# Sampled stage of a hybrid decoder step: the second state's decay and update moved ahead of the first state's product

## Time and profile before

| | us |
|---|---|
| median of 3 runs (lowest, highest) | 1473.77 (1472.54, 1475.15) |
| the profiled execution, its own time | 1470.45 |
| its span, first to last instruction | 1467.6 |
| its mean granted TensorE clock | 0.948 of full speed |
| PE, DVE, ACT, POOL busy in the whole span | 1335.7, 943.5, 638.4, 299.7 |
| the sampled stage: first load issued, next stage's first | 804.17, 858.14 |

### The profile page before, as it was taken

One profiled execution on the slowest core, in us unless ns is written; L12 is line 12 of the kernel. 1 busy time (PEld: TensorE's weight loads), 2 busy tenths in 40 slices (PEclk: granted clock), 3 DMA queues, 4 the chain that ended last, 5 costly groups with the idle time before them and its releaser, 6 DMA issues. The chain is left out here.

```text
span 1467.6 us, 22290 instructions
## 1 busy us (share of the span) xinstructions
PE 1335.7 (91%) x8165; PEld 1195.9 (81%) x8165; DVE 943.5 (64%) x1328; ACT 638.4 (43%) x960; POOL 299.7 (20%) x320
## 2 busy tenths in 40 slices
PE   7999999999999978999998859999937999999990
PEld 5999999999999978998998627888726888888870
DVE  4579766611245345777676667656278999989973
ACT  6331211122220023444543343333126888888874
POOL 0011111100000004636471000000002333333321
PEclk9999999999999988999999759999958999999995
DMA  5011112232111146272532654342154989999938
GB/s 217 29 44 33 53 58 90 93 109 90 64 56 60 49 109 168 60 139 61 115 63 67 262 178 162 122 130 77 68 190 164 268 265 264 273 271 278 284 58 290
DMA packets 118684, 199.21 MB, mean 136 GB/s; under 512 B 64412, under 2 KB 89244, under 8 KB 113732
## 3 DMA queue, kind: packets, MB, share of 16 engines
q1 hardware_dynamic: 103028, 140.70, 31.0%
q0 software_dynamic: 15568, 57.37, 14.0%
HBM read 202.12 MB, written 49.41 MB: 171 GB/s over the span
## 5 line engine op out<-in xcount | busy, mean ns | idle before, releaser
L98 PE MATMUL c_ps<-hn_lo,c_whi 128*128 128x368 f32 x936 | 177.5, 332 | 0.0
L98 PE MATMUL c_ps<-hn_hi,c_wlo 128*128 128x368 f32 x936 | 176.7, 331 | 0.0
L98 PE MATMUL c_ps<-hn_hi,c_whi 128*128 128x368 f32 x936 | 176.7, 331 | 0.0
L2349 DVE TENSOR_TENSOR e_winlo<-e_win,e_winhi 128x2048 fp32r<-128x2048 f32 x66 | 151.1, 2291 | 21.8 <-ACT e_winhi L2277 19.9
L98 PEld LDWEIGHTS c_ps<-hn_lo,c_whi 128*128 128x128 f32 x936 | 159.4, 188 | 4.8 <-issue 4.8
L98 PEld LDWEIGHTS c_ps<-hn_hi,c_wlo 128*128 128x128 f32 x936 | 159.9, 188 | 0.0
L98 PEld LDWEIGHTS c_ps<-hn_hi,c_whi 128*128 128x128 f32 x936 | 159.9, 188 | 0.0
L82 ACT CAST c_whi<-near 128x1024 fp32r<-128x1024 f32 x40 | 41.9, 1048 | 216.5 <-PE c_ps L98 216.5
L2277 ACT CAST e_winhi<-e_win 128x2048 fp32r (+1 forms) x66 | 122.8, 1917 | 3.9 <-DMA e_win<-in_w_gate_up 2.8
L2190 POOL DMA_INDIRECT x_rows<-e_ys,idx_out x33 | 81.7, 2476 | 146.2 <-ACT e_ys L2302 146.2
L603 DVE SCALAR_TENSOR_TENSOR c_y<-c_raw,c_taps,c_y 128x1128 f32<-128x1128 f32 x60 | 83.7, 1394 | 7.0 <-DVE c_y L599 2.1
(11 more groups left out here) (508 smaller groups left out, 2683.8 us busy)
## 6 DMA issues: line engine op xcount, KB each, us to landing
e_win<-in_w_gate_up SPq DMA_DIRECT2D x33, 2048.0 KB
e_wdn<-in_w_down SPq DMA_DIRECT2D x33, 1024.0 KB
near<-in_w_in SPq DMA_DIRECT2D x40, 512.0 KB, 3.5
rc_eb<-g_rows SPq DMA_DIRECT2D x10, 1040.0 KB, 6.0
o_land<-in_w_out SPq DMA_DIRECT2D x8, 768.0 KB, 6.7
x_rows<-o_land POOLq DMA_DIRECT2D x12, 512.0 KB, 4.9
near<-g_rows SPq DMA_DIRECT2D x10, 507.0 KB
kv<-in_xT SPq DMA_DIRECT2D x4, 1104.0 KB, 9.7
```

Of the source, the lines that this page charges most:

```text
L98: mm = pe.matmul(dst, left(x, k), right(z, k), start=(n == 0 and k == 0), stop=(n == 2 and k == ks - 1))
L2349: dve.tensor_tensor(win_r[1][:, r % 2, ks, :], landed(win, here)[:, ks, :], win_r[0][:, r % 2, ks, :].bitcast(F32), ALU.subtract).then_inc ...
```

## The change

The program's results and instructions stay the same; the order on three queues (SP, PE, DVE) and the choice of banks change.

- SP loads `SS` first, then `S`, then `skip`.
- PE does `sy_state` and three of the four update product pairs (`sds0_0`, `sds1_0`, `sds0_1`) right after the products `m4` and `r1`, ahead of `states`; the fourth pair (`sds1_1`) comes after the product `w`.
- DVE does `yst`, `ss_decayed` and three of the four pairs of adds right after `sspread`, ahead of `rhs`; the fourth (`ss1_1`) comes after the spreads.
- Update product `sds1_0` writes banks 2 and 3 instead of 0 and 5. So `sy` on PE waits for `ss1_0`, the product `w` for `ss0_1`, `sds1_1` for `ss0_0`; `ds0` and `ds1` lose their waits on `ss1_0` and `ss0_1`.

```
--- before.py
+++ after.py
@@ -1285,11 +1285,11 @@
                              range(g * HP, (g + 1) * HP)).then_inc(p.sem, 1)
 
 
-SAM_PE = ["kk", "k", "v", "qk", "m2", "m2t", "xt", "bt", "cb", "m4", "r1", "states", "r2", "sy", "w", "sy_state",
-          "sds0_0", "sds1_0", "sds0_1", "sds1_1", "o", "y"] + [f"ds{h}" for h in range(HA)]
+SAM_PE = ["kk", "k", "v", "qk", "m2", "m2t", "xt", "bt", "cb", "m4", "r1", "sy_state", "sds0_0", "sds1_0", "sds0_1",
+          "states", "r2", "sy", "w", "sds1_1", "o", "y"] + [f"ds{h}" for h in range(HA)]
 SAM_DVE = ["sub_b", "neg_b", "sub_k", "sub_q", "sub_s", "neg_k", "neg_qs"] + [f"fan{h}" for h in range(HA)] + [
-           "m", "mt", "r0", "vb", "qkt", "c_fan", "m2t", "kd", "xdt", "xdd", "cbt", "r1", "sspread", "rhs", "r2", "w"] + [
-           f"spread{h}" for h in range(HA)] + ["yst", "ss_decayed", "ss0_0", "ss1_0", "ss0_1", "ss1_1", "o", "sy"] + [
+           "m", "mt", "r0", "vb", "qkt", "c_fan", "m2t", "kd", "xdt", "xdd", "cbt", "r1", "sspread", "yst", "ss_decayed", "ss0_0", "ss1_0", "ss0_1",
+           "rhs", "r2", "w"] + [f"spread{h}" for h in range(HA)] + ["ss1_1", "o", "sy"] + [
            f"s{h}" for h in range(HA)]
 SAM_ACT = ["dec", "eb", "dec_t", "egt0", "egt1", "m2", "bt", "m4", "o_state"] + [f"decayed{h}" for h in range(HA)]
 SAM_POOL = ["clear", "clear_c"]
@@ -1356,7 +1356,7 @@
         sy_state_ps = bank[1][:, 0:W].rearrange("p (h t) -> p h t", h=HPG)
         full, ident, neg_t, neg = masks[:, 0, :], masks[0:L, 0, 0:L], masks[0:L, 4, 0:L], masks[0:L, 5, 0:L]
         dec_s, dec_q, dec_k = dec_t[:, 0:HB], dec_t[:, HB:HB + HA], dec_t[:, HB + HA:]
-        SDS, DS = (((4, 6), (0, 5)), ((1, 7), (4, 6))), ((0, 5), (1, 7), (2, 3), (4, 6))
+        SDS, DS = (((4, 6), (2, 3)), ((1, 7), (4, 6))), ((0, 5), (1, 7), (2, 3), (4, 6))
         halves = [slice(i * HALF * LSEQ, (i + 1) * HALF * LSEQ) for i in range(2)]
 
         def over(mask, n):
@@ -1380,9 +1380,9 @@
         @block.sync
         def _(sp):
             wait = waiter(sp)
+            sp.dma_start(SS[:], io["state_ssd"]).then_inc(sstate_moved, 16)
             sp.dma_start(S[:], io["state_gdn"]).then_inc(state_moved, 16)
             sp.dma_start(skip[:], io["d_skip"]).then_inc(skip_loaded, 16)
-            sp.dma_start(SS[:], io["state_ssd"]).then_inc(sstate_moved, 16)
             mixing.load_early(sp)
             sp.wait_ge(sstate_moved, 16)
             def of_pass(ap, i):
@@ -1501,6 +1501,25 @@
                 ins = dve.tensor_tensor(sspread[:, g], flat.to_broadcast([L, HALF, W]),
                                         seq_in_half[:].unsqueeze(2).to_broadcast([L, HALF, W]), ALU.mult)
             ins.then_inc(v.sem, 1)
+            wait(a, "egt1")
+            wait(p, "sy_state")
+            tt_(yst[:], sy_state_ps, bc(egt[:], PB), ALU.mult)
+            last = eb[:, R_SSD:R_Q, :].rearrange("p h (b t) -> p b h t", t=LSEQ)[:, :, :, LSEQ - 1:LSEQ]
+            tt_(SS[:], SS[:], last.to_broadcast([P, NSEQ, HB, PB]), ALU.mult)
+            wait(v, "ss_decayed")
+
+            def add_ss(i, g):
+                wait(p, f"sds{g}_{i}")
+                for half in range(2):
+                    b = HALF * half + 2 * i
+                    new = SS[:, b:b + 2, g * HPG:(g + 1) * HPG, :]
+                    ins = dve.tensor_tensor(new, bank[SDS[i][g][half]][:].rearrange("p (b h t) -> p b h t", b=2, t=PB),
+                                            new, ALU.add)
+                ins.then_inc(v.sem, 1)
+
+            add_ss(0, 0)
+            add_ss(0, 1)
+            add_ss(1, 0)
             wait(v, "vb")
             wait(a, "o_state")
             tt_(rhs[:], vb[:], ost[0:L], ALU.subtract)
@@ -1513,21 +1532,7 @@
             for h in range(HA):
                 tt_(spread[:, h], w[:, h, :].unsqueeze(1).to_broadcast([L, HALF, DK]),
                     seq_in_half[:].unsqueeze(2).to_broadcast([L, HALF, DK]), ALU.mult)
-            wait(a, "egt1")
-            wait(p, "sy_state")
-            tt_(yst[:], sy_state_ps, bc(egt[:], PB), ALU.mult)
-            last = eb[:, R_SSD:R_Q, :].rearrange("p h (b t) -> p b h t", t=LSEQ)[:, :, :, LSEQ - 1:LSEQ]
-            tt_(SS[:], SS[:], last.to_broadcast([P, NSEQ, HB, PB]), ALU.mult)
-            wait(v, "ss_decayed")
-            for i in range(2):
-                for g in range(GB):
-                    wait(p, f"sds{g}_{i}")
-                    for half in range(2):
-                        b = HALF * half + 2 * i
-                        new = SS[:, b:b + 2, g * HPG:(g + 1) * HPG, :]
-                        ins = dve.tensor_tensor(new, bank[SDS[i][g][half]][:].rearrange("p (b h t) -> p b h t", b=2, t=PB),
-                                                new, ALU.add)
-                    ins.then_inc(v.sem, 1)
+            add_ss(1, 1)
             wait(p, "o")
             dve.tensor_copy(queries, tall(2)).then_inc(v.sem, 1)
             wait(p, "y")
@@ -1582,6 +1587,28 @@
             wait(v, "m2t")
             prod(sq_(7), m2t, m2)
             prod(sq_(5), m2, r0)
+            pe.wait_ge(sstate_moved, 16)
+            wait(v, "kd")
+            for b in range(NSEQ):
+                for g in range(GB):
+                    at = (g * NSEQ + b) * L
+                    mm = pe.matmul(sy_state_ps[g * L:(g + 1) * L], c_fan[:, at:at + L], SS[:, b, g * HPG:(g + 1) * HPG, :],
+                                   start=(b == 0), stop=(b == NSEQ - 1))
+            mm.then_inc(p.sem, 1)
+
+            def add_products(i, g):
+                for half in range(2):
+                    mm = pe.matmul(bank[SDS[i][g][half]][:], bt[halves[half], g, :],
+                                   sspread[halves[half], g, 2 * i:2 * i + 2].rearrange("p b t -> p (b t)"),
+                                   start=True, stop=True)
+                mm.then_inc(p.sem, 1)
+
+            wait(v, "sspread")
+            wait(a, "m4")
+            add_products(0, 0)
+            add_products(0, 1)
+            wait(v, "yst")
+            add_products(1, 0)
             pe.wait_ge(state_moved, 16)
             for h in range(HA):
                 wait(v, f"fan{h}")
@@ -1593,7 +1620,7 @@
             wait(a, "m4")
             wait(v, "r1")
             prod(sq_(5), m4, r1)
-            wait(v, "cbt")
+            wait(v, "ss1_0")
             for h in range(HB):
                 half = slice((h % 2) * PB, (h % 2 + 1) * PB)
                 mm = pe.matmul(tall(3)[half, h // 2, :], xdt[:, h, :], cbt[:, h, :], start=(h < 2), stop=False,
@@ -1601,28 +1628,10 @@
             mm.then_inc(p.sem, 1)
             wait(v, "rhs")
             wait(v, "r2")
+            wait(v, "ss0_1")
             prod(wide(7), r2, rhs)
-            pe.wait_ge(sstate_moved, 16)
-            wait(v, "kd")
-            for b in range(NSEQ):
-                for g in range(GB):
-                    at = (g * NSEQ + b) * L
-                    mm = pe.matmul(sy_state_ps[g * L:(g + 1) * L], c_fan[:, at:at + L], SS[:, b, g * HPG:(g + 1) * HPG, :],
-                                   start=(b == 0), stop=(b == NSEQ - 1))
-            mm.then_inc(p.sem, 1)
-            wait(v, "sspread")
-            wait(a, "bt")
-            for i in range(2):
-                for g in range(GB):
-                    if (i, g) == (1, 0):
-                        wait(v, "yst")
-                    if (i, g) == (1, 1):
-                        wait(v, "ss0_0")
-                    for half in range(2):
-                        mm = pe.matmul(bank[SDS[i][g][half]][:], bt[halves[half], g, :],
-                                       sspread[halves[half], g, 2 * i:2 * i + 2].rearrange("p b t -> p (b t)"),
-                                       start=True, stop=True)
-                    mm.then_inc(p.sem, 1)
+            wait(v, "ss0_0")
+            add_products(1, 1)
             wait(v, "w")
             for h in range(HA):
                 pe.matmul(tall(2)[:, h, :], w[:, h, :], qkt[:, h, :], start=(h == 0), stop=False, skip_group_check=True)
@@ -1639,7 +1648,8 @@
             mm.then_inc(p.sem, 1)
             for h in range(HA):
                 wait(v, f"spread{h}")
-                wait(v, ("ss1_0", "ss0_1", "sy", "ss1_1")[h])
+                if h >= 2:
+                    wait(v, ("sy", "ss1_1")[h - 2])
                 for half in range(2):
                     mm = pe.matmul(bank[DS[h][half]][:], kd[halves[half], h, :],
                                    spread[halves[half], h].rearrange("p b t -> p (b t)"), start=True, stop=True)
```

## The result

The changed kernel takes 1466.35 us (median of 7 runs, 1464.18 to 1468.87), the kernel before 1473.77 (7 runs): ratio 0.9948, interval 0.9935 to 0.9960. That is 7.4 us less, where 7.6 were forecast. The trace shows that the agreement is better than the working behind it.

What follows compares the result with a forecast made beforehand. The prediction took the sampled stage to end with the first state's stores, started by `s0`. It summed 20.1 - 6.3 - 6.2 = 7.6 us, all else 0, so 1473.77 - 7.6 = 1466.2 us; range 1463.3 to 1470.8.

Steps and rivals of the forecast that it cites:

- The end hangs on `s0` and 7.4 us of stores: End of the stage: the first state's four stores run unbroken for 7.4 us, so when `s0` is done sets the end.
- rival C: First state's stores: they are no limit, the end follows `s3`; gain 9.5 us, 1464.3 us, chance 0.05.
- 6.2 us of work put ahead of `states`: TensorE: `sy_state` (3.60 us) and three update pairs (2.6 us) make everything to the copy of `w` 6.2 us later.
- 6.3 us in place of 20.1 in the tail: VectorE, end of the copy of `w` to end of `s0`: 6.3 us instead of 20.1, without waiting for TensorE.
- Does the clock hold?: TensorE to `ds1`: longest gap 0.82 us, so the clock was taken to stay at 1.00.
- rival A: TensorE's tail: the clock is low all the same; gain 4.3 us, 1469.5 us, chance 0.13.
- What hides the moved work: VectorE ahead of `rhs`: 7.16 us idle plus 6.2 us of delay cover the moved work, 2 us to spare; no cost.
- the new waits: TensorE's waits for `ss1_0`, `ss0_1` and `ss0_0`: all over in time, 0 us.
- the loads: SP's loads: `SS`, issued first, lands at 812.1 against 815.6 when wanted; `S` and `skip` also in time; 0 us.
- rival D: SP's loads: `SS` lands as late as before, `sy_state` starts at 817.1; gain 6.1 us, 1467.7 us, chance 0.04.
- B: TensorE: the clock doesn't rise while `sy_state` runs; 8.7 us slower, 1482.5 us, chance 0.04.
- E: Next stage or a misread wait: the earlier end is given back, no difference; 1473.8 us, chance 0.08.

## Why the prediction was right, and where it was not

- **The end hangs on `s0` and 7.4 us of stores:** right. The stores took 7.3 us in the changed kernel. With the two small extra matmuls VectorE's last add ended at 842.16 + 4.88 = 847.04, 6.0 us ahead of the next stage (853.04), and the stores still took 7.4 us. The rate for 512 bytes stayed at 285 GB/s against 368 to 396 for 4 KB, so the sentence of the Trainium skill, "DMA: Bandwidth & Descriptors", section "Specifications", on line rate from 512 bytes was not borne out here: rival C did not come.
- **6.2 us of work put ahead of `states`:** right in size. The copy of `w` came 6.0 to 6.7 us later in the five traces, and the clock rose 14.5 to 15.5 us after the stage's start in all of them, so at the same moment, as the working assumed. `sy_state` took 5.48 us because its first part ran at the low clock, `states` 7.41 instead of 9.22, as the same low stretch fell on the other.
- **6.3 us in place of 20.1 in the tail:** the step that failed, by 1.9 us: 8.0 to 8.4 us were measured. Its basis was "Does the clock hold?", which reckoned that without the gap that preceded the fall the clock stays. The gap went, TensorE was busy for the 3.2 us ahead of the fall, and the clock fell all the same. That is rival A, in a milder form: it reckoned the whole of `sds1_1`, `o` and `y` at the low clock (tail 9.6 us, gain 4.3); the fall came in the middle of `o`. With the clock held by extra matmuls the tail was 6.3 us, so the reckoning of the work itself was right.
- **What hides the moved work, the new waits, the loads, the decays:** right. 2.25 us were left ahead of `rhs` (2 forecast), TensorE waits for no add into the second state, `SS` was there in time. The price of the load order if it had not been (1.5 us, rival D) was measured as 1.5.
- **The sum:** 7.6 us forecast, 5.6 us in the stage, 7.4 us in the medians. The median landed on the forecast by luck: two misses cancel. The profiled execution took 1465.21 us where 1462.9 were forecast, 2.3 us more, 2.0 of them in the stage. And the step from it to the median, "I take the same difference", did not hold: the median lay 3.3 us above the profiled execution before and 1.1 us above it in the changed kernel, which gives 2.2 us back. Whether that is scatter outside the stage or something that no trace shows is open. Two sums on rivals are slightly off, and nothing hangs on them: C less the scatter of the runs is 1463.0 and not 1463.3, and C's gain is counted against an end of 857.5, which stands in no row (the data ended at 857.25, the stage at 858.14). Rivals B and E did not come.

## What to carry to other kernels

Before moving work into an engine's idle time, follow the PSUM banks: here the new deal of two banks decides between 5.6 us gained and 2 us lost. A clock that is up in the trace before is a term of the sum, not a given: what was priced at the full clock behind a gap has to be priced at both levels even if the gap goes. Where a stage ends in a row of stores that follow each other without a hole, look for what starts the first of them, not for what ends the last. And a median that is forecast from one profiled execution carries that execution's place among the runs: here it was worth 2.2 us, against a change of 7.4.

## What was not expected of the hardware

The granted TensorE clock fell from 1.00 to 0.50 (2.4 to 1.2 GHz) with TensorE busy without a gap for the 3.2 us ahead of it, on matmuls of 64 to 128 columns and a few of 512 with 32 rows; two more matmuls of 128x384 and 128x256 kept it at 1.00 in each of three traces. An fp32 matmul of 128 rows by 512 columns took about 1 us at the high clock (1.98 for two); six of 32 rows by 512 columns took 2.84. Stores with the DMA engines full moved 282 to 285 GB/s in pieces of 512 bytes, 341 in pieces of 1 KB and 396 in pieces of 4 KB.
